# Modulation rows in column-group matmuls, most of them fetched during layer 0's attention

## The reference, cut to what matters

```python
m  = (silu_c  @ w_mod[l] + b_mod[l])      # (6*1024), for latent tokens
mc = (silu_cc @ w_mod[l] + b_mod[l])      # the same for context tokens
h  = rms_norm(x, g_pre_mix[l]) * (1.0 + sc1) + sh1
y, yc = token_mixer(h, hc, p, ...)        # h @ w_in, then four head groups, then @ w_out
x = x + gt1 * rms_norm(y, g_post_mix[l])
h = rms_norm(x, g_pre_mlp[l]) * (1.0 + sc2) + sh2
x = x + gt2 * rms_norm(sq_relu_mlp(h, w1, w2), g_post_mlp[l])
```

## Time and profile before

| | us |
|---|---|
| median of 3 runs | 2789.66 (2784.95 to 2791.29) |
| the profiled execution | 2786.89 |
| its span, first to last instruction | 2785.1 |
| PE busy | 2471.6 (89%) |
| DVE, POOL, ACT busy | 1074.8, 785.0, 704.3 |
| mean granted TensorE clock | 0.943 |
| modulation matmuls, 384 records | 175.1 |

### The profile page before, as it was taken

One profiled execution on the slowest core, in us unless ns is written; L12 is line 12 of the kernel. 1 busy time (PEld: TensorE's weight loads), 2 busy tenths in 40 slices (PEclk: granted clock), 3 DMA queues, 4 the chain that ended last, 5 costly groups with the idle time before them and its releaser, 6 DMA issues.

```text
span 2785.1 us, 52373 instructions
## 1 busy us (share of the span) xinstructions
PE 2471.6 (89%) x22294; PEld 1919.4 (69%) x22294; DVE 1074.8 (39%) x1615; ACT 704.3 (25%) x1169; POOL 785.0 (28%) x556
## 2 busy tenths in 40 slices
PE   7899888987778989999999899987987778899997
PEld 1288756755776668888888327865765766688886
DVE  2300156546344463323232430036636344634433
ACT  0110135453232121111112011124454232212221
POOL 0133135002102322323233114305302103444444
PEclk9999899998899979999999999989997899899998
DMA  7611000000001011111111562000000002122221
GB/s 263 237 53 53 0 1 0 0 20 2 4 4 62 30 46 61 61 65 63 60 61 65 172 238 80 30 1 1 0 20 2 4 4 77 53 98 91 98 98 60
DMA packets 45171, 162.78 MB, mean 58 GB/s; under 512 B 5504, under 2 KB 5504, under 8 KB 44768
## 3 DMA queue, kind: packets, MB, share of 16 engines
q1 hardware_dynamic: 43328, 152.89, 16.2%
q0 software_dynamic: 1696, 7.67, 0.8%
HBM read 158.45 MB, written 2.10 MB: 58 GB/s over the span
## 4 chain that ended last, share of the span: by engine, by line
PE 75%; DVE 12%; issue 7%; ACT 4%; POOL 1%; DMA 0%; SPq 0%; ACTq 0%; DVEq 0%; POOLq 0%
PE ps L1246 72%; PE ps L1454 2%; DVE xT L924 1%; DVE small L1019 1%; DVE flat L1230 1%; DVE hT L892 1%; DVE flat L995 1%; DVE flat L992 1%; POOL flat L468 1%; DMA flat<-wmod_dram 0%; PE ps L1706 0%; DVE part_h L912 0%; DVE flat L922 0%; DVE flat L1129 0%; DVE hT L906 0%
## 5 line engine op out<-in xcount | busy, mean ns | idle before, releaser
L1246 PE MATMUL ps<-part_hi,wparts 128*128 128x512 f32 (+1 forms) x3072 | 811.6, 352 | 23.0 <-DVE part_lo L1232 7.9
L1246 PE MATMUL ps<-flat 64*64 64x32 f32 (+8 forms) x9112 | 569.2, 269 | 129.6 <-DVE flat L1119 30.1
L1246 PEld LDWEIGHTS ps<-part_hi,wparts 128*128 128x128 f32 x3072 | 542.3, 190 | 110.4 <-DVE part_h L897 12.5
L1246 PEld LDWEIGHTS ps<-flat 64*64 64x64 f32 (+3 forms) x9112 | 434.9, 160 | 252.1 <-issue 130.5
L449 POOL TENSOR_TENSOR wparts<-flat,wparts 128x1024 fp32r<-128x1024 f32 x184 | 441.9, 2401 | 545.5 <-ACT wparts L836 539.7
L1246 PE MATMUL ps<-part_h,wparts 128*128 128x512 f32 (+1 forms) x1344 | 473.2, 352 | 0.0
L1246 PE MATMUL ps<-part_mlp,wparts 128*128 128x512 f32 (+1 forms) x1536 | 417.9, 359 | 11.5 <-DVE part_h L912 11.5
L1246 PE MATMUL ps<-part_lo,wparts 128*128 128x512 f32 x960 | 340.6, 355 | 0.0
L1246 PEld LDWEIGHTS ps<-part_mlp,wparts 128*128 128x128 f32 x1536 | 275.6, 191 | 60.2 <-DVE part_h L912 11.6
L836 ACT ACTIVATE wparts<-flat 128x1024 fp32r<-128x1024 f32 x112 | 118.8, 1061 | 705.0 <-PE ps L1246 705.0
L1246 PEld LDWEIGHTS ps<-part_h,wparts 128*128 128x128 f32 x1344 | 257.1, 191 | 32.0 <-issue 0.5
(11 more groups left out here) (195 smaller groups left out, 2203.2 us busy)
## 6 DMA issues: line engine op xcount, KB each, us to landing
flat<-w_dram SPq DMA_DIRECT2D x128, 512.0 KB, 3.5
flat<-wmod_dram SPq DMA_DIRECT2D x96, 512.0 KB, 4.4
flat<-win_dram SPq DMA_DIRECT2D x40, 512.0 KB, 3.5
flat<-wout_dram SPq DMA_DIRECT2D x16, 512.0 KB, 4.1
xT<-xT_dram SPq DMA_DIRECT2D x8, 384.0 KB, 7.3
flat<-rope_dram POOLq DMA_DIRECT2D x2, 1024.0 KB, 5.3
out_dram<-xT SPq DMA_DIRECT2D x8, 256.0 KB, 2.0
flat<-wmask_dram POOLq DMA_DIRECT2D x2, 768.0 KB, 6.8
```

The costliest lines, as they stand in the source:

```text
L1246: return pe.matmul(out, lhsT, rhs, start=start, stop=stop)
```

## The change

1. **Which rows when.** Four column tiles (`MOD_FIRST`: shift and scale of layer 0's mixer) are computed at the start, the other 20 (`MOD_REST`, eight of layer 0 and twelve of layer 1) inside layer 0's attention: four in each latent iteration, two in each context iteration.
2. **How.** `silu` is widened to 32 columns for each k (two real, 30 zero). In `modulate` the matmuls of slab q write partitions 32q to 32q+31 of one bank, so that four column groups of the array hold four slabs; two rounds of four matmuls make a column tile. The sum over the four groups is taken in `mod_columns`, where each 128-wide piece of the row block is the stationary operand against a 128 x 2 matrix of ones (`pick`).
3. **Where in the attention.** After `turns(10)` PE runs half of the iteration's column tiles, after `turns(11)` the other half, each before `output(h)`. `modulate` waits for all four slabs of its tile. ACT copies each bank as 128 x 512 (`mod_rows`). After the last head PE runs `mod_columns`, and DVE copies the result to `modT`.
4. **First norms** of both layers are built as the MLP's: squares on ACT, sums on POOL, gain and inverse root in one DVE instruction, shift on ACT. In layer 1 PE runs 22 `keep_clock` matmuls before `ssq(1, 0)`.
5. **Queues.** `xT` is loaded before the first slabs. The rope tables and their neighbours are issued by SP after the projection's slabs, and then the 80 slabs of the remaining modulation. POOL waits for `s_modT` only before the token shift. Offsets and the other seven gains are formed on DVE before layer 0's scan.

```diff
             for l in range(DEPTH):
-                stream(wmod_d, l * NMOD, NMOD // 4)
                 if l == 0:
                     for k in range(KT):
                         sp.dma_start(xv[:, k, :], xT_d[:, k, :]).then_inc(s_x, 16)
-                stream(wmod_d, l * NMOD + NMOD // 4, 3 * NMOD // 4)
-                if l == 0:
+                    stream(wmod_d, 0, MOD_FIRST * SLOTS)
                     sp.dma_start(zT[:, 0:NKM], constm_d).then_inc(s_maskraw, 16)
                 stream(win_d, l * NZ, NZ)
+                for dst, src in ((rope, rope_d), (wmask, wmask_d), (uq, uq_d[l]), (ukv, ukv_d[l])):
+                    sp.dma_start(dst, src).then_inc(s_atab, 16)
+                if l == 0:
+                    stream(wmod_d, MOD_FIRST * SLOTS, MOD_REST * SLOTS)
...
+        def mods_in(l, b0):
+
+            if l:
+                return 0, 0
+            return (4, 0) if b0 == 0 else (2, 4 * NBL)
...
-                pool.wait_ge(s_modT, l + 1)
-                for dst, src in ((rope, rope_d), (wmask, wmask_d), (uq, uq_d[l]), (ukv, ukv_d[l])):
-                    pool.dma_start(dst, src).then_inc(s_atab, 16)
+                sum_squares(l, 0)
...
+                def mod_rows(first, n, bank_at, row, col):
+
+                    act.wait_ge(s_used[SLOTS - 1], 1 + first + n + 1)
+                    nc_.activation(row[:, col * 512:(col + 1) * 512], ps[:, bank_at * 512:(bank_at + 1) * 512],
+                                   ACT.Copy).then_inc(s_modrow, 1)
+
+                squares(l, 0, xv)
+                if l == 0:
+                    for n in range(MOD_FIRST):
+                        if n == 2:
+                            root(0, NB)
+                        mod_rows(0, n, n, modrow[0], n)
+                else:
+                    root(4 * l, NB)
                 first_parts(l, 0)
...
                         for h in range(12):
                             turned(h)
                             if h < 10:
                                 exps(h + 2)
+                            elif mods_n:
+                                if h == 10:
+                                    act.wait_ge(s_modps, i + (b0 + 1))
+                                for j in range(mods_n // 2):
+                                    col = (h - 10) * (mods_n // 2) + j
+                                    mod_rows(i * mods_n + (F_REST + mods_at), col, 2 * (h - 10) + j, modrow[1], col)
...
+                inverse_root(4 * l, TOK)
+                if l == 0:
+
+                    dve.wait_ge(s_maskraw, 16)
+                    V.tensor_copy(km[:, :], zT[:, 0:NKM]).then_inc(s_masks, 1)
+                    dve.wait_ge(s_modps, 1)
+                    ch.link(V.tensor_copy(modT[:, 0:8 * MOD_FIRST], ps[:, MOD_AT[0]:MOD_AT[0] + 8 * MOD_FIRST]))
+                    offsets(0, 0, 4 * MOD_FIRST)
+                    ch.link(gain_of(0, 0))
+                normed_parts(l, 0)
...
+                if l == 0:
+                    dve.wait_ge(s_modc, NB)
+                    offsets(0, 4 * MOD_FIRST, NMOD)
+                    offsets(1, 0, NMOD)
+                    for m, n in ((0, 1), (0, 2), (0, 3), (1, 0), (1, 1), (1, 2), (1, 3)):
+                        ins = gain_of(m, n)
+                    ch.link(ins)
...
+            def modulate(first, n, bank_at):
+
+                for q in range(SLOTS):
+                    pe.wait_ge(s_slab[q], first * 16 + 16 * (n + 1))
+                for j in range(2):
+                    for q in range(SLOTS):
+                        ins = mm(ps[32 * q:32 * q + 32, bank_at * 512:(bank_at + 1) * 512], siluv[:, 2 * q + j, :],
+                                 slab[:, q * SLAB + j * 512:q * SLAB + (j + 1) * 512], j == 0, j == 1)
+                        if j:
+                            ins.then_inc(s_used[q], 1)
+
+            def mod_columns(row, n, at):
+
+                for m in range(4 * n):
+                    ins = mm(ps[:, at + 2 * m:at + 2 * m + 2], row[:, m * P:(m + 1) * P], pick[:, :])
+                ins.then_inc(s_modps, 1)
...
-                modulation(0)
-                ssq(l, 0)
-                modulation(6)
-                pe.wait_ge(s_modrow, 1 + 12 * (l + 1))
-                for m in range(NMOD):
-                    ins = pe.transpose(ps[:, 3584 + 2 * m:3586 + 2 * m], work[0:2, m * P:(m + 1) * P], ident[0:2, 0:2])
-                ins.then_inc(s_modps, 1)
-                keep_clock(0, 11)
+                if l == 0:
+                    for n in range(MOD_FIRST):
+                        if n == 2:
+                            ssq(0, 0)
+                        modulate(0, n, n)
+                    fills[0] += MOD_FIRST
+                    pe.wait_ge(s_modrow, MOD_FIRST)
+                    mod_columns(modrow[0], MOD_FIRST, MOD_AT[0])
+                    keep_clock(0, 7)
+                else:
+                    keep_clock(0, 22)
+                    ssq(l, 0)
...
                             turns(h)
                             if h < 10:
                                 scores(h + 2)
+                            elif mods_n:
+                                for j in range(mods_n // 2):
+                                    modulate(i * mods_n + (fills[0] + mods_at), (h - 10) * (mods_n // 2) + j,
+                                             2 * (h - 10) + j)
                             output(h)
-
+                        if mods_n:
+                            pe.wait_ge(s_on, 1 + it * 12 + 11)
+                            pe.wait_ge(s_modrow, i * mods_n + (MOD_FIRST + mods_at + mods_n))
+                            mod_columns(modrow[1], mods_n, MOD_AT[1])
```

More of the change, by code:

```diff
@@ L41 @@
 FFG = 4
[L43 to L46, removed]
+MOD_FIRST = 4
+MOD_REST = DEPTH * NMOD // SLOTS - MOD_FIRST
+PER_LAYER = (NZ + KT + 2 * FFG * KT) // SLOTS
+F_REST = MOD_FIRST + NZ // SLOTS
+F_IN = tuple(MOD_FIRST + l * (MOD_REST + PER_LAYER) for l in range(DEPTH))
+F_OUT = tuple(MOD_FIRST + MOD_REST + l * PER_LAYER + NZ // SLOTS for l in range(DEPTH))
+F_MLP = tuple(f + KT // SLOTS for f in F_OUT)
 T_OUT = NZ // SLOTS
@@ L122, in backbone @@
         cT = sb("cT", KT * 2)
-        silu = sb("silu", KT * 2)
-        modT = sb("modT", NMOD * 2)
-        gain = sb("gain", 4 * 16)
+        silu = sb("silu", KT * 32)
+        pick = sb("pick", 2)
+        modT = sb("modT", DEPTH * NMOD * 2)
+        gain = sb("gain", DEPTH * 4 * 16)
         omm = sb("omm", 32)
@@ L135, in backbone @@
         zv = zT[:, :].rearrange("p (k t) -> p k t", k=NZ)
[L136 to L137 removed]
+        mods = modT[:, :].rearrange("p (l k s) -> p l k s", l=DEPTH, s=2)
+        gains = gain[:, :].rearrange("p (l n k s) -> p l n k s", l=DEPTH, n=4, s=2)
+        siluv = silu[:, :].rearrange("p (k m) -> p k m", k=KT)
         ident, ones, bd = (kf[:, k * P:(k + 1) * P] for k in (K_ID, K_ONES, K_BD))
@@ L577, in _ @@
             act.wait_ge(s_eps, 1)
-            nc_.activation(silu[:, :], cT[:, :], ACT.Sigmoid).then_inc(s_silu, 1)
+            nc_.activation(siluv[:, :, 0:2], cT[:, :].rearrange("p (k s) -> p k s", s=2), ACT.Sigmoid).then_inc(s_silu, 1)
             def squares(l, which, src):
-                t = TOK if l < DEPTH - 1 else LAT
+                t = TOK if which == 0 or l < DEPTH - 1 else LAT
                 for k in range(KT):
-                    if which == 2:
+                    if which == 0 and l == 0:
+                        act.wait_ge(s_x, 16 * KT)
+                    elif which == 0:
+                        act.wait_ge(s_xup, 16 * l - KT + k + 1)
+                    elif which == 2:
                         act.wait_ge(s_xup, 16 * l + k + 1)
@@ L598, in first_parts @@
                     act.wait_ge(s_xn, 16 * l + 4 * which + k + 1)
[L599 to L604, removed]
+                    for s, a, b in segs(l, which == 2):
+                        ins = nc_.activation(pre_hi[which][:, k, a:b], hv[:, k, a:b], ACT.Identity,
+                                             bias=mods[:, l, 12 * which + k, s:s + 1])
                     ins.then_inc(s_h, 1)
             for l in range(DEPTH):
[L609 to L613, removed]
-                modulation(0)
-                root(4 * l, NB)
-                modulation(6)
+                def mod_rows(first, n, bank_at, row, col):
[10 more added lines that the diff above has]
+                    root(4 * l, NB)
                 first_parts(l, 0)
@@ L885, in inverse_root, with offsets, gain_of, normed_parts @@
                 dve.wait_ge(s_rs, n + 1)
[L887 removed]
+            def offsets(l, first, last):
+                ch.link(V.tensor_tensor(mods[:, l, first:last], mods[:, l, first:last],
+                                        pars(l, "b_mod", last - first, first).unsqueeze(2).to_broadcast([P, last - first, 2]),
+                                        ALU.add))
+            def gain_of(l, n):
+                name, part, plus = (("g_pre_mix", 8, 1), ("g_post_mix", 16, 0), ("g_pre_mlp", 32, 1), ("g_post_mlp", 40, 0))[n]
```

(8 more changed lines are left out.)

107 lines of the change are left out of this document (37 added, 70 removed).

## The result

The changed kernel takes 2839.1 us (median of 4 runs, 2833.1 to 2846.9), the kernel before 2789.8 (2785.0 to 2791.3): ratio 1.018, 95% interval 1.015 to 1.021. It is slower by 49 us; 2860 was forecast, with 2800 to 2915 as the range. The profiled execution of the changed kernel spans 2836.4 us at a mean granted clock of 0.914; before it was 2785.1 at 0.943.

The account below looks back on a forecast made before the run. PE was taken as the bound, with 75% of the chain and no DMA in it. From 2786.9 us, the starts -73.2 and -53.1, attention +167.6 and +30.4, small terms +1.6 gave 2860 us, range 2800 to 2915.

Parts of the forecast that it names:

- the refill: Four modulation slabs freed together and wanted together: 9.2 us from last use until all are back, lower bound about 7.4.
- `mod_columns`: Column matmuls after the tiles: 32 two-column records at 0.20 us each, 6.4 us; 16 records in context iterations, 3.2 us.
- the tails: Ends of layer 0's attention iterations: +41.9 us per latent one, four times +168; +15.2 per context one, twice +30.
- Layer 1's start: Layer 1 from its `x` update to the first projection tile: tile out at 1605.9 instead of 1679.1, -73 us.
- Layer 0's start: Layer 0 up to its first projection tile: out at 92.4 us instead of 145.5, -53 us.
- Four column groups at once: A column tile's matmuls run in four array column groups together: 1.75 us instead of 7.03, 3.45 after a cold wait.
- The rival in which they run one after another: Column groups don't run at once: a modulation takes 7.0 us, about 8.5 from cold; total 2895 us, chance 0.12.
- the kinder rival: Refill 7.4 us, clock full through waits, two-column records at 0.125 us: total 2780 us, faster than before; chance 0.12.

Follow-up runs that it names:

- the run that keeps the clock: Changed kernel plus eight identity matmuls ahead of each of the 14 attention column tiles that wait for slabs: 2814.9 us.
- the spread kernel: Changed kernel with the attention's column tiles placed one at a time behind output(h) of several heads instead of at each iteration's end: 2743.4 us, ratio 0.984.

## Why the prediction was right, step by step

The sign, the mechanism and the order of the terms were right: the waits for slabs freed together, in PE's in-order queue, outweigh both starts. The sum came out 21 us too high. Two prices, the refill and `mod_columns`, made the tails 26 us too long; 11 us of slower work outside the tails, which the sum had at nothing, went the other way, and some 4 came back behind the attention.

- **Layer 1's start**, -73.2 forecast, -72.6 measured. It was read from the MLP norm in the same trace, and the low parts end 52.3 us after the update begins, as in the model.
- **Layer 0's start**, -53.1 forecast, -52.5 measured. Within it the slabs came 0.7 us earlier than assumed, the third tile earlier (its slabs came during the norm's sums), and the columns took 6.99 instead of 6.4. They ended at 66.8 instead of 68.4; from there to the first tile it took 26.3 us instead of 24.0. That the total is so close is luck: two errors cancelled.
- **The refill**, 9.2 us in the sum, was 7.6 to 8.4 in the attention (end of one modulation to the start of the next; in the first iteration 7.71, 8.22, 7.68), and 8.84, 7.72 and 8.60 at the start. The four latent iterations are together about 16 us short of the forecast by it, the two context ones 2. SP issued the four DMAs within 1.6 us in both places; what differs is the last landing. From issue to landing, of the first refill at the start and of the first in the attention:

```profile
DMA to landing us min/median/max: 3.5/5.2/7.0
...
DMA to landing us min/median/max: 3.6/4.7/5.8
```

  Why it lands later in some refills than in others, no run shows. The 6.8 us by the page "DMA: Bandwidth & Descriptors" of the Trainium skill (Anatomy of one DMA) stay below all of them; the page gives its figure for DMAs issued by gpsimd, while these slabs are issued by SP.
- **`mod_columns`**, 6.4 us in the sum, took 4.28, 4.53, 4.88 and 4.65 in the four latent iterations, and 1.95 and 3.41 for the 16 records of the context ones: 8 us less than the forecast together. 0.20 us a record was read at the half clock of the earlier trace rows. The price was right for that clock (6.99 us at layer 0's start, granted clock 0.50; 3.63 at 1.00 in the run that keeps the clock), and I put it into stretches with another, 0.83 in the first one.
- **Four column groups at once**, 1.75 at full clock and 3.45 at half: 1.92 and 3.64. The rival in which they run one after another fell with the first row, and by its bound from rows of other shapes it was rightly held small. The page "TensorEngine Tiling (Array Packing)" of the Trainium skill (Available Configurations) has four independent column tiles; the trace agrees, with 16 records in 1.92 us, the first four of them begun within the first 0.04 us of the tile. Its drain on a change of mode is no term here: what follows a tile starts within 0.1 us of its modelled end.
- **The tails**: latent +41.9 forecast, +36.2 measured; the two context iterations +15.2 each forecast, about +13 and +15 measured. The waits are 7.7, 6.2 and 7.7 us and one of 7.1 or 7.4, against "about 9, 6.5 and 9". The attention, forecast to go from 214 to about 410 us, went from 220 to 403.
- **What the sum left out.** The next two scores take 5.47 us instead of the 2.82 of the earlier trace rows; the attention grew by 183 us, the tails by 172. This is not the slab waits' cold clock reaching on: the granted clock was back at 1.00 in the column matmuls and fell again behind them. The changed kernel first; then the spread kernel, where no slab is waited for; then the run without the attention's tiles:

```profile
413.00:415.00 2.00, 2.00 (x20) 2.00 (x20) 0.28 (x1) 1.93 (x6) 0.00 (x0) 1.00 0.96 379
416.00:420.00 4.00, 4.00 (x11) 2.78 (x11) 0.29 (x2) 0.00 (x0) 0.00 (x0) 0.50 0.50 203
...
451.00:455.00 4.00, 4.00 (x16) 3.48 (x16) 0.19 (x1) 0.00 (x0) 3.78 (x7) 0.50 0.18 72
...
418.55 2.82 PE L1268 MATMUL ps<-flat 128*128 128x512 f32 x8 [0.96 <-ACT flat L685]
```

  In the spread kernel these scores take 4.3 to 4.5 us. So the loss goes with the column matmuls and not with the waits; that they cause it is argued, as no run leaves them out alone.
- **What comes back.** Behind the attention 3.9 us come back, where the stretch to `wout`'s first issue takes 236.6 instead of 240.5 us: the 48 two-column records that follow the attention took 9.19 us behind a wait of 2.94 for ACT, and now take 5.42, without that wait:

```profile
741.30 5.42 PE L1270 MATMUL ps<-kf,flat 128*128 128x2 f32 x48
```

- **A slip in a rival.** The sum of the kinder rival leaves the 0.9 us of `output(11)` out of its two context iterations: 2782 us instead of 2780. Nothing hangs on it.

Together: the attention and what follows, up to `wout`'s first issue, cost 179 us instead of 199.6, and the starts brought 125 instead of 126.3. That is +54; the spans differ by 51, and the 3 us between lie elsewhere.

## What to carry to other kernels

When several buffers of a ring are freed by one step and wanted together by the next, the step costs a whole refill, whatever its own work is. Ask first how long that refill is, with the way to the DMA and back (about 3 of 7.7 us here), then put that much other work between two such steps, or use and free the buffers singly: twenty tiles at the ends of the iterations cost 174 us, the same tiles spread over the heads 78, and 60 with their copies hidden. A gain at a start is worth what the place that takes the work over leaves of it.

## What I had not expected of the hardware

- Column groups do not wait for each other in program order: with both matmuls of a group side by side, 16 records of four groups took 1.94 us, and 1.92 with the groups alternating.
- A refill of four 64 KB slabs took 3.8 us and one of four 512 KB slabs 7.7; eight times the bytes are only twice the time.
- The same 32 two-column records took 3.63, 4.28 and 6.99 us, at a granted clock of 1.00, 0.83 and 0.50: very small matmuls follow the clock like large ones.
- The granted clock fell to 0.50 in or behind such records although PE was at work. In the run that keeps the clock, PE was busy throughout and the clock at 1.00 from 553 to 557 us, and at 0.50 from 558 to 563; the column matmuls of that iteration took 4.98 us instead of 3.63.
- A wait of 3.8 us of PE was in one place enough to have all of the next 16 records slow, in another only part of them; in the same run one tile behind 2.9 us of waiting took 1.92 us and another 3.40.
